# Gathering the overflow rows of four experts as one group of 128

## The chip, the cores and the metric

One Trainium2 chip, of which this kernel uses one core. The core has TensorE (matrix products, with a separate instruction that loads the stationary operand), VectorE, ScalarE, GpSimd and SyncE, which run their own instruction streams and wait for each other through semaphores, and 16 DMA engines. The metric is the device time of one launch in microseconds (us). An engine name in a profile row is short: PE is TensorE's products, PEld its loads of stationary operands, DVE is VectorE, ACT ScalarE, POOL GpSimd, SP SyncE.

## The reference, cut to what matters

One decoder layer on 1024 tokens of width 1024: forgetting attention, a layer norm, a mixture of experts, a layer norm. The change touches the mixture of experts: 64 experts, 8 for each token, each with a gate and an up matrix of 1024 x 256 and a down matrix of 256 x 1024, and one shared expert of the same size that takes all tokens.

```python
def moe(x, w_router, router_bias, w_gate, w_up, w_down, ws_gate, ws_up, ws_down):
    ...
    _, top_e = lax.top_k(jnp.where(exp_mask, sel, -jnp.inf), TOP_K)
    w = jnp.take_along_axis(scores, top_e, axis=-1)
    w = w / jnp.sum(w, -1, keepdims=True) * ROUTED_SCALE
    ...
    # for each block of rows of one expert e:
        xb = x_pad[rows]
        h = jax.nn.silu(xb @ w_gate[e]) * (xb @ w_up[e])
        yb = (h @ w_down[e]) * rw[:, None].astype(xb.dtype)
        acc = acc.at[rows].add(yb)
    shared = (jax.nn.silu(xf @ ws_gate) * (xf @ ws_up)) @ ws_down
```

An expert has 128 tokens on the mean (8192 choices, 64 experts), some have more and some fewer.

## The kernel before, in words

All products are made in a split form: a float32 operand is written as a high part (what the product's number format keeps) and a low part (the rest), and a product is the sum of high x high, high x low and low x high. The high part is a copy on ScalarE, the low part a subtraction on VectorE.

**Tables.** After routing, every choice of a token is written into a table in device memory (`tab_dram`). For each expert the table has a column for its first 128 tokens and then columns for blocks of 32 further tokens; a column stands for 128 rows of which a further block uses 32. `TAB_BLOCKS` = 29 columns lie side by side for each expert (`e * TAB_BLOCKS + k`), and SyncE reads the whole table into SBUF (L548, 928 KB). Places of no token hold the numbers of rows that are zero. `further` has the number of further blocks of each expert, `earlier` the number of further blocks of all experts before it.

**One expert.** GpSimd gathers its 128 rows (1024 values and 64 token weights for each, 4352 bytes) with an indirect DMA (L657) some three experts ahead. TensorE turns them (eight transposes, L1015), ScalarE and VectorE split them (L1424, L1922). The weights come by plain DMA in four pieces for gate and up (L493) and two for down (L498), 512 KB each, are split piece by piece (L1396 on ScalarE, L1918 on VectorE), and are held in two sets. TensorE makes the gate and up products in 16 + 8 matmuls (`gate_up`, L1025, L1028, L1031), two transposes of h (L1039), and the down product in 12 (`down`, L1052, L1053, L1060). ScalarE scales the result by the tokens' weights (L1444), and GpSimd adds it to the sums in device memory with an accumulating indirect DMA (`add_first`, L682). Each add waits for the add before it.

**A further block** of 32 rows is gathered on its own (`gather_further`, L670), turned on its own (`turn_further`, eight transposes, L1074), copied into `xo` by ScalarE (`further_rows_hi`, L1486) and VectorE (`further_rows_lo`, L1938): columns 0 to 31 of `xo` are the high part, 32 to 63 the low part, the rest is zero. Then TensorE makes 16 matmuls with the same gate and up weights (`gate_up_further`, L1084, L1085), and in the next expert two transposes (L1093) and eight matmuls of the down product (L1102, L1103).

**The order on TensorE**, written out by hand, for expert e (m = e + 8, since the shared expert's eight tiles come first): transposes of h of e - 1; gate and up of e; if e - 1 had a further block, its two transposes; the turning of the rows of e + 1 into `q_ps`; if e - 1 had a further block, its down product; if e has one, its turning; the down product of e - 1 into `k_ps`; if e has a further block, its gate and up product. ScalarE and VectorE follow the same order: of the four weight pieces of a coming expert VectorE does three, then h of e, then the fourth, then the split of the next rows, then the two pieces of the down weights. The loops of the engines have two experts in a turn. In the end the last expert's results are not added through memory but placed by TensorE (L1118 to L1128), together with a second layer norm.

Of the kernel before, what the change touches and what calls it, by code (L numbers as in the profile page):

```python
# [73 lines left out]
XR = P // 4  # L74

# [20 lines left out]
def build(nc, x, w_in, b_f, w_out, ln1_g, ln1_b, router, router_bias, w_gate, w_up, w_down, ws_gate, ws_up,  # L96
          ws_down, ln2_g, ln2_b, out):
    with ExitStack() as ctx:
# [135 lines left out]
        with ExitStack() as m:  # L234
# [6 lines left out]
            xo = sb("xo", [P, DC, P], F32R, c=m)  # L241
# [16 lines left out]
            tab = sb("tab", [P, TAB], I32, c=m)  # L258
            tok_f = sb("tok_f", [P, 1], c=m)
            tok_x = sb("tok_x", [2 * XR, 1], c=m)  # L260
        with ExitStack() as f:
# [18 lines left out]
            sb("up_to_the_other_set", [P, 19240], c=f)  # L280
# [5 lines left out]
        for n in ("masks xt_ps xt_hi_ok xt_lo_ok wf_in wf_ok gate_ps g1_in gate_step zexp_ok"  # L286
# [7 lines left out]
                  " ht_lo_ok downed scaled w_ok x_in x_turned x_rows_hi_ok x_rows_lo_ok x_w_ok x_gated x_half x_sum x_silu_ok x_h_ok x_ht_ps x_ht_hi_ok x_ht_lo_ok"  # L294
                  " x_downed x_y_half x_scaled ax_ok ax_stored summed"
                  " stands std_ok var_ok place_step y_hi_ok f_placed f_pair f_mean f_var f_std f_scaled f_step f_xg f_out").split():
# [17 lines left out]
        w_rows = w_in.rearrange("(c p) n -> p c n", p=P)  # L314
        v_rows = v_dram.rearrange("(t p) h n -> p t h n", p=P)
# [64 lines left out]
        def _(sp):  # L380
# [166 lines left out]
            sp.wait_ge(S["extra_ok"], 2)  # L547
            sp.dma_start(tab[:], tab_dram.rearrange("(p n) o -> p (n o)", p=P)).then_inc(S["c_loads"], 16)  # L548
# [36 lines left out]
        def _(pool):  # L585
# [27 lines left out]
            g.iota(e8[:], pattern=[[TAB_BLOCKS, E]], base=1, channel_multiplier=0, allow_small_or_imprecise_dtypes=True).then_inc(S["c_const"], 1)  # L613
# [26 lines left out]
            def wait_routed():  # L640
                pool.wait_ge(S["listed"], 16 * TT * TOP_K)
                pool.wait_ge(S["extra_ok"], 2)
                pool.wait_ge(S["x1_stored"], 16 * TT)
                pool.wait_ge(S["wts_stored"], 16 * TT)

            def gather(i, e, count, free):
# [5 lines left out]
                g.tensor_copy(gidx[i][:], tab[:, ds(e * TAB_BLOCKS, 1)]).then_inc(idx_ok[i], 1)  # L652
# [19 lines left out]

            def add_first(par, e):
# [3 lines left out]
                g.tensor_copy(sidx[par][:], tab[:, ds(e * TAB_BLOCKS, 1)]).then_inc(S["sidx_ok"], 1)  # L677
# [7 lines left out]
            def add_further(e, k, x):  # L685
                pool.wait_ge(sent[2], 16 * x + SENT_0[2])
                stand(pool)
                g.tensor_copy(sidx[2][0:XR], tab[0:XR, ds(e * TAB_BLOCKS + k + 1, 1)]).then_inc(S["x_sidx_ok"], 1)
# [4 lines left out]
                                     in_=ys[2][0:XR], in_offset=None, compute_op=ALU.add).then_inc(sent[2], 16)  # L693

            def earlier_of(e):
                return pool.value_load(earlier[0:1, ds(e + 1, 1)], min_val=0, max_val=E * TAB_BLOCKS)

# [3 lines left out]
            for b in range(SH):  # L701
# [11 lines left out]
            f0, f1 = further_of(0), further_of(1)  # L713
            with pool.If(f0 > 0):
                gather_further(0, 0, 0, 0)
            with pool.If(f0 < 2):
# [1438 lines left out]
```

## Time and profile before

| | |
|---|---|
| median of 3 runs | 1633.97 us (1632.95 to 1635.86) |
| the profiled execution | 1633.34 us, span of its instructions 1631.7 us |
| TensorE | busy 1567.5 us (96%) |
| TensorE's loads | 1309.8 us (80%) |
| VectorE | 1178.9 us (72%) |
| ScalarE | 1033.5 us (63%) |
| GpSimd | 506.6 us (31%) |
| data moved by DMA | 368.63 MB |

Busy time is the union of the instructions' times on that engine. Matmuls are pipelined: a matmul of 512 columns is shown with about 0.39 us, while the next one begins 0.23 us after it. Expert 0 begins at 752 us of the span, expert 63 at 1568.

### The profile page before, as it was taken

Reading aid. Unit: us, or ns where it says so; the run is one execution under the profiler, and the core shown is the slowest. Engines: PE = TensorE matmul, PEld = TensorE weight load, DVE = VectorE, ACT = ScalarE, POOL = GpSimd, SP = SyncE. Lnnn points to the kernel's source line nnn. Section 1 sums busy time; section 2 is a strip of 40 time slices with the busy share of each in tenths; the row PEclk is TensorE's granted clock in tenths of the full one; section 3 lists DMA queues with packets and bytes.
Section 4 is the critical chain, followed back from the end, with each engine's and each line's share of the span. In section 5 each row is a group of like instructions: output and inputs, shape, how many; then the busy total and the mean of one; then the engine's idle time right before and its main releaser. Section 6 shows DMA issues by size and latency. Waiting matters only on the chain.

```text
span 1631.7 us, 32189 instructions
## 1 busy us (share of the span) xinstructions
PE 1567.5 (96%) x8246; PEld 1309.8 (80%) x8247; DVE 1178.9 (72%) x2037; ACT 1033.5 (63%) x1706; POOL 506.6 (31%) x495
## 2 busy tenths in 40 slices
PE   6999999999999999989999999999999999999986
PEld 6897888888887788778888888888888888888763
DVE  4215777777777788836877787777876787888866
ACT  3215666666666654526777787767776777878754
POOL 0000000000000125532554454543454454454426
PEclk9999999999999999999999999999999999999995
DMA  7223322222123434557999999999999999999987
GB/s 246 91 81 91 72 53 65 58 64 71 45 71 104 161 144 146 221 192 267 330 312 323 304 354 366 342 289 274 333 328 286 286 358 327 352 367 362 368 250 281
DMA packets 161321, 368.63 MB, mean 226 GB/s; under 512 B 53010, under 2 KB 73490, under 8 KB 161266
## 3 DMA queue, kind: packets, MB, share of 16 engines
q1 hardware_dynamic: 136272, 284.21, 49.7%
q0 software_dynamic: 24992, 83.73, 19.7%
q8 instruction: 28, 0.46, 0.1%
q14 instruction: 29, 0.22, 0.0%
HBM read 294.39 MB, written 65.11 MB: 220 GB/s over the span
## 4 chain that ended last, share of the span: by engine, by line
PE 73%; DVE 8%; DMA 7%; issue 5%; ACT 3%; ACTq 2%; POOL 1%; SPq 0%; DVEq 0%; POOLq 0%
PE bank_pair L1031 6%; PE bank_pair L1025 6%; PE bank_pair L1028 6%; DMA sums_scratch<-ys,sidx 6%; PE q_ps L91 4%; PE q_ps L93 4%; PE q_ps L92 4%; PE out_ps L916 4%; PE k_ps L894 3%; PE out_ps L1084 3%; PE out_ps L1085 3%; PE q_ps L1015 3%; PE k_ps L1052 2%; PE k_ps L1053 2%; PE k_ps L1060 2%
## 5 line engine op out<-in xcount | busy, mean ns | idle before, releaser
L1918 DVE TENSOR_TENSOR gu_lo<-raw_gu,gu_hi 128x1024 fp32r<-128x1024 f32 x260 | 306.4, 1220 | 28.0 <-ACT gu_hi L1396 27.8
L1396 ACT CAST gu_hi<-raw_gu 128x1024 fp32r<-128x1024 f32 x260 | 253.6, 1049 | 7.1 <-DMA raw_gu<-in_moe_w_up_dram 7.1
L1025 PE MATMUL bank_pair<-gu_hi,xb_hi 128*128 128x512 f32 x576 | 233.9, 406 | 5.3 <-DVE gu_lo L1918 3.9
L1028 PE MATMUL bank_pair<-gu_lo,xb_hi 128*128 128x512 f32 x576 | 227.7, 395 | 0.0
L682 POOL DMA_INDIRECT sums_scratch<-ys,sidx x63 | 120.8, 1917 | 152.9 <-DMA sums_scratch<-ys,sidx 118.9
L1918 DVE TENSOR_TENSOR dn_lo<-raw_dn,dn_hi 128x1024 fp32r<-128x1024 f32 x130 | 152.6, 1213 | 2.8 <-ACT dn_hi L1396 2.3
L1031 PE MATMUL bank_pair<-gu_hi,xb_lo 128*128 128x512 f32 x576 | 144.0, 392 | 3.8 <-DVE xb_lo L1922 3.8
L1025 PEld LDWEIGHTS bank_pair<-gu_hi,xb_hi 128*128 128x128 f32 x576 | 110.6, 192 | 28.6 <-issue 5.8
L613 POOL IOTA e<- 128x64 f32 x1 | 0.2, 185 | 427.5 <-DVE xs L1714 427.5
L1396 ACT CAST dn_hi<-raw_dn 128x1024 fp32r<-128x1024 f32 x130 | 130.0, 1052 | 4.2 <-DMA raw_dn<-in_moe_w_down_dram 4.2
L1301 ACT CAST pt_hi<-k_ps 128x512 fp32r<-128x512 f32 (+1 forms) x192 | 85.8, 482 | 73.5 <-PE k_ps L894 72.8
L1031 PEld LDWEIGHTS bank_pair<-gu_hi,xb_lo 128*128 128x128 f32 x576 | 108.5, 188 | 26.9 <-DVE xb_lo L1922 4.3
L1028 PEld LDWEIGHTS bank_pair<-gu_lo,xb_hi 128*128 128x128 f32 x576 | 110.1, 191 | 21.3
L657 POOL DMA_INDIRECT x_rows<-rows_scratch,gidx x64 | 80.5, 1258 | 140.7 <-DVE wcol L1934 109.1
L1692 DVE TENSOR_TENSOR pt_lo<-k_ps,pt_hi 128x512 fp32r<-128x512 f32 (+1 forms) x192 | 100.3, 550 | 27.4 <-ACT pt_hi L1301 26.6
L1052 PE MATMUL k_ps<-dn_hi,ht_hi 128*128 128x512 f32 x288 | 118.3, 411 | 0.0
L1053 PE MATMUL k_ps<-dn_lo,ht_hi 128*128 128x512 f32 x288 | 112.6, 391 | 0.0
L91 PE MATMUL q_ps<-xt_hi,wqk_hi 128*128 128x512 f32 x256 | 108.8, 425 | 0.0
L1290 ACT ACTIVATE probs<-bank_pair,nm 128x512 f32<-128x512 f32 (+3 forms) x128 | 74.8, 587 | 43.2 <-DVE nm L1685 29.8
L1084 PE MATMUL out_ps<-gu_hi,xo 128*128 128x512 f32 x248 | 97.3, 392 | 4.8 <-DVE xo L1938 4.8
L93 PE MATMUL q_ps<-xt_hi,wqk_lo 128*128 128x512 f32 x256 | 100.3, 392 | 0.0
L92 PE MATMUL q_ps<-xt_lo,wqk_hi 128*128 128x512 f32 x256 | 100.0, 391 | 0.0
(307 smaller groups left out, 3967.5 us busy)
## 6 DMA issues: line engine op xcount, KB each, us to landing
raw_gu<-in_moe_w_gate_dram SPq DMA_DIRECT2D x128, 512.0 KB, 7.0
raw_gu<-in_moe_w_up_dram SPq DMA_DIRECT2D x128, 512.0 KB, 9.1
raw_dn<-in_moe_w_down_dram SPq DMA_DIRECT2D x128, 512.0 KB, 8.7
wqk<-in_fox_w_in_dram SPq DMA_DIRECT2D x66, 128.0 KB, 2.5
v_scratch<-v_out SPq DMA_DIRECT2D x32, 256.0 KB, 2.8
va<-v_scratch SPq DMA_DIRECT2D x16, 512.0 KB, 4.6
fin<-sums_scratch SPq DMA_DIRECT2D x16, 512.0 KB, 9.5
xs<-in_x_dram SPq DMA_DIRECT2D x8, 512.0 KB, 7.3
```

Source lines behind the costliest of these rows:

```text
L91: pe.matmul(out, w_hi, m_hi, start=start, stop=False, skip_group_check=True)
L92: pe.matmul(out, w_hi, m_lo, start=False, stop=False, skip_group_check=True)
L93: return pe.matmul(out, w_lo, m_hi, start=False, stop=stop, skip_group_check=True)
L682: g.indirect_dma_start(out=sums[0], out_offset=bass.IndirectOffsetOnAxis(ap=sidx[par][:, 0:1], axis=0), in_=ys[par][:], in_offset=None, co ...
L1025: i = pe.matmul(o3, xb_hi[s][:, c], g_hi[:, :, c], start=c == 0, stop=False, skip_group_check=True)
L1028: pe.matmul(o3, xb_hi[s][:, c], g_lo[:, :, c], start=False, stop=False, skip_group_check=True)
L1031: i = pe.matmul(o3, xb_lo[s][:, c], g_hi[:, :, c], start=False, stop=c == DC - 1, skip_group_check=True)
L1052: pe.matmul(k_ps[:, r], ht_hi[:, c], d_hi[:, c, r], start=c == 0, stop=False, skip_group_check=True)
L1053: pe.matmul(k_ps[:, r], ht_hi[:, c], d_lo[:, c, r], start=False, stop=False, skip_group_check=True)
L1084: pe.matmul(o3, xo[:, c], g_hi[:, :, c], start=c == 0, stop=False, skip_group_check=True)
L1396: a.copy(hi, raw).then_inc(S[done], 1)
L1918: dve.tensor_tensor(lo, raw, hi, ALU.subtract).then_inc(S[lo_ok], 1)
```

## The change

The first further blocks of four consecutive experts are one group. GpSimd gathers 4 x 32 rows with one indirect DMA of 128 rows (`gather_four`), for each of the 16 groups, whether its experts have a further block or not; places of no block read the zero rows. In the first expert of a group (j = 0) TensorE turns all 128 rows with the eight full transposes into `k_ps` (`turn_four`), between the eighth and the ninth matmul of gate and up; before that it waits for the gather and for the scaling that last read `k_ps`. ScalarE copies the high part between its third and fourth weight piece (`rows_of_four_hi`), VectorE subtracts the low part after its third piece and copies the four columns of weights (`rows_of_four_lo`), and TensorE waits for that before it writes `k_ps` again in the down product. `xo` now holds all four experts, each as 32 columns of high and 32 of low part for each of the eight chunks; the stationary operand of a further product is 128 columns from the expert's place on, so that its last 64 columns are rows of a neighbour, whose results nobody reads. Second and later further blocks of an expert go another way (`gather_again`, `turn_again`), with their table column read from device memory.

The table is laid out by block (column `k * E + e`), so that only its first 128 columns, 64 KB, are read into SBUF. VectorE makes one more running sum (`again`, second and later blocks) and four small copies that put the groups' indices together (`fidx`). The loops have four experts in a turn. Several semaphores are merged.

```diff
-            xg = [sb(f"x_rows{i}", [P, ROW_W], c=m) for i in range(3)]
+            xg = [sb(f"x_rows{i}", [P, ROW_W], c=m) for i in range(2)]
+            xgx = sb("x_rows_of_four", [P, ROW_W], c=m)
...
-            ys = [sb(f"ys{i}", [P, D], c=m) for i in range(3)]
+            ys = [sb(f"ys{i}", [P, ROW_W if i == 2 else D], c=m) for i in range(3)]
+            xr = ys[2][XR:2 * XR]
...
-            tab = sb("tab", [P, TAB], I32, c=m)
+            tab = sb("tab", [P, 2 * E], I32, c=m)
+            xo = sb("xo", [P, DC * 2 * P + 2 * XR], F32R, c=m)
+            xo_of = xo[:, 0:DC * 2 * P].rearrange("p (c j s r) -> p c j s r", j=FOUR, s=2, r=XR)
+            fidx = sb("fidx", [P, E // FOUR], I32, c=m)
+            fidx_g = sb("fidx_g", [P, 1], I32, c=m)
+            w_four = sb("w_four", [P, FOUR], c=m)
+            again = sb("again", [1, E + 1], I32, c=m)
...
-            sp.dma_start(tab[:], tab_dram.rearrange("(p n) o -> p (n o)", p=P)).then_inc(S["c_loads"], 16)
+            sp.wait_ge(S["extra_ok"], 3)
+            sp.dma_start(tab[:], tab_rows[:, 0:2 * E]).then_inc(S["c_loads"], 16)
...
-            g.iota(e8[:], pattern=[[TAB_BLOCKS, E]], base=1, channel_multiplier=0, allow_small_or_imprecise_dtypes=True).then_inc(S["c_const"], 1)
+            g.iota(e8[:], pattern=[[1, E]], base=1, channel_multiplier=0, allow_small_or_imprecise_dtypes=True).then_inc(S["c_const"], 1)
...
-            def gather_further(par, e, k, x):
-
-                if not static(x):
-                    with pool.If(x > 0):
-                        pool.wait_ge(S["x_in"], 16 * x)
-                        stand(pool)
+            def gather_four(n):
+
+                if static(n) and n == 0:
+                    pool.wait_ge(S["extra_ok"], 3 + FOUR)
+                else:
+                    pool.wait_ge(S["fx_lo_ok"], 2 * n)
                 stand(pool)
-                g.tensor_copy(gidx[2][0:XR], tab[0:XR, ds(e * TAB_BLOCKS + k + 1, 1)]).then_inc(idx_ok[2], 1)
-                pool.wait_ge(idx_ok[2], x + 1)
+                g.tensor_copy(fidx_g[:], fidx[:, ds(n, 1)]).then_inc(idx_ok[2], 1)
+                pool.wait_ge(idx_ok[2], n + 1)
                 stand(pool)
-                g.indirect_dma_start(out=xg[2][par * XR:(par + 1) * XR], out_offset=None, in_=rows_dram,
+                g.indirect_dma_start(out=xgx[:], out_offset=None, in_=rows_dram,
+                                     in_offset=bass.IndirectOffsetOnAxis(ap=fidx_g[:, 0:1], axis=0)).then_inc(S["fx_in"], 16)
+
+            def gather_again(e, k, n):
+
+                pool.wait_ge(S["x_rows_lo_ok"], n + 1)
+                stand(pool)
+                pool.dma_start(gidx[2][0:XR], tab_rows[0:XR, ds((k + 1) * E + e, 1)], allow_slow_non_contiguous=True).then_inc(S["x_in"], 16)
+                pool.wait_ge(S["x_in"], 32 * n + 16)
+                stand(pool)
+                g.indirect_dma_start(out=xr, out_offset=None, in_=rows_dram,
                                      in_offset=bass.IndirectOffsetOnAxis(ap=gidx[2][0:XR, 0:1], axis=0)).then_inc(S["x_in"], 16)
...
+            gather_four(0)
...
+                if j == 1 and not (static(four) and four == E // FOUR - 1):
+                    gather_four(four + 1)
...
                 with pool.If(nx > 1):
-                    with pool.Fori(1, nx) as k:
-                        pool.wait_ge(S["x_w_ok"], xi + k + 1)
-                        gather_further(par, e, k, xi + k)
-                        add_further(e, k - 1, xi + k - 1)
-                    if not ends:
-                        with pool.If(f1 > 0):
-                            gather_further(1 - par, e + 1, 0, xi + nx)
-                if pos != "last":
-                    with pool.If(f1 < 2):
-                        with pool.If(f2 > 0):
-                            pool.wait_ge(S["x_w_ok"], xi + nx + 1)
-                            gather_further(par, e + 2, 0, xi + nx + f1)
+                    n = again_of(e)
+                    sums_rows(first_of_further(e), xi)
+                    add_further(xi)
+                    gather_again(e, 1, n)
+                    with pool.If(nx > 2):
+                        with pool.Fori(2, nx) as k:
+                            sums_rows(gidx[2][0:XR], xi + k - 1)
+                            add_further(xi + k - 1)
+                            gather_again(e, k, n + k - 1)
...
+            def gate_up(s, w, names, n, between=None):
...
+                    if between and c == DC // 2 - 1:
+                        between()
...
-            def turn_further(par, x):
-
-                pe.wait_ge(S["x_in"], 16 * x + 16)
+            def turn_four(n, m):
+
+                pe.wait_ge(S["fx_in"], 16 * n + 16)
+                pe.wait_ge(S["scaled"], m - 1)
                 stand(pe)
-                rows = slice(par * XR, (par + 1) * XR)
-                v = strided(xg[2][rows, 0:D])
+                turn_rows(xgx, k_ps).then_inc(S["fx_turned"], 1)
...
-                pe.wait_ge(S["x_rows_lo_ok"], x + 1)
                 pe.wait_ge(S["x_scaled"], x + 1)
                 for c in range(DC):
-                    pe.matmul(o3, xo[:, c], g_hi[:, :, c], start=c == 0, stop=False, skip_group_check=True)
-                    i = pe.matmul(o3, xo[:, c], g_lo[:, :, c], start=False, stop=c == DC - 1, skip_group_check=True)
-                i.then_inc(S["x_gated"], 1)
+                    rows = xo[:, (FOUR * c + j) * 2 * XR:(FOUR * c + j) * 2 * XR + P]
+                    pe.matmul(o3, rows, g_hi[:, :, c], start=c == 0, stop=False, skip_group_check=True)
+                    i = pe.matmul(o3, rows, g_lo[:, :, c], start=False, stop=c == DC - 1, skip_group_check=True)
+                i.then_inc(S["x_product"], 1)
...
+                between = None if j else rows_of_four
...
+                if j == 0:
+                    pe.wait_ge(S["fx_lo_ok"], 2 * four + 1)
+                    stand(pe)
                 with pe.If(nx > 0):
                     with pe.If(nx > 1):
+                        n = pe.value_load(again[0:1, ds(e, 1)], min_val=0, max_val=E * TAB_BLOCKS)
+                        pe.wait_ge(S["ht_lo_ok"], m)
+                        stand(pe)
                         with pe.Fori(0, nx - 1) as k:
-                            pe.wait_ge(S["ht_lo_ok"], m)
-                            turn_further(par, xi + k)
-                            gate_up_further(w, xi + k)
+                            gate_up_further(w, j, xi + k)
                             turn_h_further(xi + k)
                             down_further(w, e + 2, xi + k)
-                    pe.wait_ge(S["ht_lo_ok"], m)
-                    turn_further(par, xi + nx - 1)
+                            turn_again(n + k)
+                            pe.wait_ge(S["x_rows_lo_ok"], n + k + 2)
+                            stand(pe)
                     down(m - 1, par, e + 1)
                     if last:
...
+                        next_gate_up(m, e, par, range(G_PIECES - 1))
+                    if j == 0:
+                        rows_of_four_hi(four)
+                    if pos != "last":
+                        next_gate_up(m, e, par, range(G_PIECES - 1, G_PIECES))
...
+            def rows_of_four_hi(n):
+                act.wait_ge(S["fx_turned"], n + 1)
+                a.copy(xo[:, 0:DC * 2 * P].rearrange("p (q s r) -> p q s r", s=2, r=XR)[:, :, 0], k_ps[:].rearrange("p (q r) -> p q r", r=XR)
+                       ).then_inc(S["fx_hi_ok"], 1)
...
-                step(dve.tensor_tensor(pos_b[:], pos_b[:], e8[:], ALU.add))
+                step(dve.scalar_tensor_tensor(out=pos_b[:], in0=pos_b[:], scalar=float(E), in1=e8[:], op0=ALU.mult, op1=ALU.add))
...
+                step(dve.tensor_scalar(u[:], nblk_i[1][:], float(-(P // XR) - 1), 0.0, ALU.add, ALU.max))
+                shift = 1
+                while shift < E:
+                    step(dve.tensor_copy(v[:, 0:shift], u[:, 0:shift]))
+                    step(dve.tensor_tensor(v[:, shift:E], u[:, shift:E], u[:, 0:E - shift], ALU.add))
+                    u, v = v, u
+                    shift *= 2
+                step(dve.memset(again[:], 0))
+                dve.tensor_copy(again[:, 1:E + 1], u[:]).then_inc(S["extra_ok"], 1)
...
-            def further_rows_lo(par, e, x):
-                dve.wait_ge(S["x_rows_hi_ok"], x + 1)
-                dve.tensor_tensor(xo[:, :, XR:2 * XR], banks[1][:, FF:FF + DC * XR].rearrange("p (c t) -> p c t", c=DC), xo[:, :, 0:XR],
+            def rows_of_four_lo(n):
+                dve.wait_ge(S["fx_hi_ok"], n + 1)
+                q = xo[:, 0:DC * 2 * P].rearrange("p (q s r) -> p q s r", s=2, r=XR)
+                dve.tensor_tensor(q[:, :, 1], k_ps[:].rearrange("p (q r) -> p q r", r=XR), q[:, :, 0], ALU.subtract).then_inc(S["fx_lo_ok"], 1)
+                dve.tensor_copy(w_four[:], xgx[:, ds(FOUR * n + D, FOUR)]).then_inc(S["fx_lo_ok"], 1)
+
+            def first_weights(j, four):
+                dve.wait_ge(S["fx_lo_ok"], 2 * four + 2)
+                stand(dve)
+                dve.tensor_copy(w_x[:], w_four[j * XR:(j + 1) * XR, j:j + 1])
...
+                    dve.wait_ge(S["c_loads"], 64)
+                    for j in range(FOUR):
+                        dve.tensor_copy(fidx[j * XR:(j + 1) * XR], tab[0:XR, E + j:2 * E:FOUR]).then_inc(S["extra_ok"], 1)
...
+            with pe.Fori(0, E // FOUR - 1) as i:
+                for j in range(FOUR):
+                    expert(FOUR * i + j, j, i)
```

## Rows read from the trace of the kernel before

**Rows 1.** Windows of the expert stage: length, busy time per engine, clock, DMA share, GB/s.
```profile
785.00:1385.00 600.00, 594.86 (x2918) 496.29 (x2917) 465.64 (x594) 436.40 (x571) 292.52 (x282) 1.00 0.99 320
1385.00:1485.00 100.00, 99.06 (x486) 83.15 (x485) 84.91 (x105) 79.09 (x101) 49.08 (x45) 1.00 1.03 355
1485.00:1505.00 20.00, 19.54 (x96) 16.36 (x95) 16.92 (x21) 16.94 (x21) 10.01 (x9) 1.00 1.03 385
```

**Rows 2.** The chain that ended last, from 1480 on: first and last of ten adds.
```profile
1490.46 9.38 DMA sums_scratch<-ys,sidx
...
1583.15 6.24 DMA sums_scratch<-ys,sidx
```

**Rows 3.** ScalarE: the rows of expert 62 are scaled.
```profile
1577.63 1.12 ACT L1444 ACTIVATE ys<-k_ps,wcol 128x1024 f32<-128x1024 f32 x1 [0.80 <-PE k_ps L1060]
```

**Rows 4.** View of the tile xo: durations, first and last start; who waited.
```profile
L1084 PE MATMUL out_ps<-gu_hi,xo x248: 387/389/504, 781.8 to 1580.8; 128*128 128x512 f32 x124
...
  PE out_ps L1084: 4.8, 6
```

**Rows 5.** TensorE in order of time, experts 12 and 15: start, length, line.
```profile
914.75 0.48 PE L1025 MATMUL bank_pair<-gu_hi,xb_hi 128*128 128x512 f32 x1
...
920.30 1.05 PE L1015 MATMUL q_ps<-ident,x_rows 128*128 128x128 f32 x8
921.11 0.48 PE L1052 MATMUL k_ps<-dn_hi,ht_hi 128*128 128x512 f32 x1
...
923.03 1.08 PE L1060 MATMUL k_ps<-dn_hi,ht_lo 128*128 128x512 f32 x4
...
949.73 1.05 PE L1015 MATMUL q_ps<-ident,x_rows 128*128 128x128 f32 x8
950.71 1.06 PE L1074 MATMUL bank_pair<-ident,x_rows 32*128 32x32 f32 x8
...
953.65 1.07 PE L1060 MATMUL k_ps<-dn_hi,ht_lo 128*128 128x512 f32 x4
954.56 0.39 PE L1084 MATMUL out_ps<-gu_hi,xo 128*128 128x512 f32 x1
```

**Rows 6.** The same at expert 6, whose further rows are late.
```profile
839.30 1.07 PE L1060 MATMUL k_ps<-dn_hi,ht_lo 128*128 128x512 f32 x4
841.24 0.50 PE L1084 MATMUL out_ps<-gu_hi,xo 128*128 128x512 f32 x1 [0.87 <-DVE xo L1938]
```

**Rows 7.** Groups by line, 800 to 1550: a full 128-row split on VectorE.
```profile
L1922 DVE TENSOR_TENSOR xb_lo<-q_ps,xb_hi 128x1024 fp32r<-128x1024 f32 x57 | 69.4, 1218 | 0.0
```

**Rows 8.** TensorE, expert 16 (further block before it): its gate and up product starts.
```profile
958.35 0.48 PE L1025 MATMUL bank_pair<-gu_hi,xb_hi 128*128 128x512 f32 x1
```

**Rows 9.** VectorE, the same expert: its three weight pieces.
```profile
961.12 3.50 DVE L1918 TENSOR_TENSOR gu_lo<-raw_gu,gu_hi 128x1024 fp32r<-128x1024 f32 x3 [0.47 <-ACT gu_hi L1396]
```

**Rows 10.** TensorE, expert 48 (no further block before it).
```profile
1396.25 0.48 PE L1025 MATMUL bank_pair<-gu_hi,xb_hi 128*128 128x512 f32 x1
```

**Rows 11.** VectorE, expert 48: its three weight pieces.
```profile
1401.33 3.50 DVE L1918 TENSOR_TENSOR gu_lo<-raw_gu,gu_hi 128x1024 fp32r<-128x1024 f32 x3 [0.52 <-ACT gu_hi L1396]
```

**Rows 12.** TensorE, expert 0.
```profile
752.08 0.48 PE L1025 MATMUL bank_pair<-gu_hi,xb_hi 128*128 128x512 f32 x1
```

**Rows 13.** GpSimd at that time: the gather for expert 2.
```profile
755.07 1.00 POOL L657 DMA_INDIRECT x_rows<-rows_scratch,gidx  x1 [0.86 <-POOL gidx L652]
```

**Rows 14.** View of the tile x_rows, 755 to 757: that gather alone.
```profile
DMA to landing us min/median/max: 5.6/5.6/5.6
```

**Rows 15.** Windows around a stop of TensorE, columns as in the first group.
```profile
703.00:707.00 4.00, 0.47 (x3) 0.04 (x1) 1.04 (x2) 0.00 (x0) 0.29 (x2) 1.00 0.97 331
707.00:711.00 4.00, 3.69 (x13) 2.94 (x14) 0.80 (x3) 0.39 (x1) 3.08 (x4) 0.66 0.09 30
```

**Rows 16.** View of the tile raw_gu, 1385 to 1420: weight pieces.
```profile
DMA to landing us min/median/max: 8.3/13.6/19.9
```

**Rows 17.** Groups by line, VectorE, 714 to 719: the running sum of block counts.
```profile
L1909 DVE TENSOR_TENSOR nblk<-nblk 1x63 f32<-1x63 f32 (+5 forms) x6 | 1.2, 203 | 0.2
```

More of the change, by code:

```diff
@@ L74 @@
 XR = P // 4
+FOUR = P // XR
 BIAS_TILES = TT // 2
@@ L762, in expert @@
                 return xi, nx
-            expert(0, 0, "first")
-            expert(1, 1, "")
-            with pool.Fori(1, E // 2 - 2) as i:
-                for par in range(2):
-                    expert(2 * i + par, par, "")
-            expert(E - 4, 0, "")
-            expert(E - 3, 1, "", ahead=False)
-            expert(E - 2, 0, "last", ahead=False)
-            xi, nx = expert(E - 1, 1, "last", ahead=False)
+            for j in range(FOUR):
+                expert(j, j, 0, "" if j else "first")
+            with pool.Fori(1, E // FOUR - 1) as i:
+                for j in range(FOUR):
+                    expert(FOUR * i + j, j, i, "")
+            for j in range(FOUR):
+                expert(E - FOUR + j, j, E // FOUR - 1, "" if j < 2 else "last", ahead=j < 1)
             for what, t in LAST_POOL:
@@ L1163, in _, with expert @@
                     logits(TT - 1)
-            def expert(e, par, last=False):
+            def expert(e, j, four, last=False):
+                par = j % 2
                 w = 1 - par
@@ L1217, in expert @@
                 return xi, nx
-            with pe.Fori(0, E // 2 - 1) as i:
-                for par in range(2):
-                    expert(2 * i + par, par)
-            expert(E - 2, 0)
-            expert(E - 1, 1, last=True)
+            with pe.Fori(0, E // FOUR - 1) as i:
+                for j in range(FOUR):
+                    expert(FOUR * i + j, j, i)
+            for j in range(FOUR):
+                expert(E - FOUR + j, j, E // FOUR - 1, last=j == FOUR - 1)
         @block.scalar
@@ L1514, in load_counts, with expert @@
                 return [act.value_load(earlier[0:1, ds(e + k, 1)], min_val=0, max_val=E * TAB_BLOCKS) for k in range(4)]
-            def expert(e, par, pos, counts):
+            def expert(e, j, four, pos, counts):
+                par = j % 2
                 m = SH + e
@@ L1585, in expert, with four_experts @@
                     a.copy(bank_pair[:], b2[:]).then_inc(S["y_hi_ok"], 1)
-            counts = load_counts(0)
-            expert(0, 0, "first", counts)
-            expert(1, 1, "", counts)
-            with act.Fori(1, E // 2 - 1) as i:
-                counts = load_counts(2 * i)
-                for par in range(2):
-                    expert(2 * i + par, par, "", counts)
-            counts = load_counts(E - 2)
-            expert(E - 2, 0, "", counts)
-            expert(E - 1, 1, "last", counts)
+            def four_experts(e0, four):
+                for j in range(FOUR):
+                    if j % 2 == 0:
+                        counts = load_counts(e0 + j)
+                    pos = "first" if static(e0) and e0 + j == 0 else "last" if static(e0) and e0 + j == E - 1 else ""
+                    expert(e0 + j, j, four, pos, counts)
+            four_experts(0, 0)
+            with act.Fori(1, E // FOUR - 1) as i:
+                four_experts(FOUR * i, i)
+            four_experts(E - FOUR, E // FOUR - 1)
             for t in range(TT):
@@ L2007, in load_counts, with expert @@
                 return [dve.value_load(earlier[0:1, ds(e + k, 1)], min_val=0, max_val=E * TAB_BLOCKS) for k in range(4)]
-            def expert(e, par, counts, last=False):
+            def expert(e, j, four, counts, last=False):
+                par = j % 2
                 m = SH + e
```

175 lines of the change are left out of this document (98 added, 77 removed).

## The prediction

> **What bounds the kernel now.** The change works in the expert stage alone, so I read that stage first: the windows from 785 to 1385 and from 1385 to 1485 [rows 1]. TensorE is busy for 595 of 600 us and for 99 of 100 at full clock, VectorE and ScalarE for 70 to 85%. Busy time of a pipelined engine proves little alone, so I then read TensorE's timeline, where a missing matmul shows as a start that is late. There the matmuls follow each other at their usual distance, with few stops. So in this stage TensorE's instruction stream sets the time, and a microsecond less on it is worth one, as long as nothing else comes up behind it. Two things stand close behind. DMA has a share of 0.99 to 1.03 and moves 320 to 385 GB/s [rows 1]; and from 1490 us on the chain that ended last has left TensorE and is ten accumulating adds, one after the other, 9.4 us for the first, to 1589.4 [rows 2]. The rows of expert 62 are scaled at 1578.75 [rows 3], and their add starts at 1583.15, because the one before it has only then landed: 4.4 us of slack for TensorE. So the end of the stage is set by when that chain starts, and what TensorE saves or loses after expert 53 is not on the path.
>
> How many blocks there are: 248 matmuls of L1084, eight for each block, are 31 blocks [rows 4]. In TensorE's timeline each of the 31 groups is followed by the next expert's products, none by a second block of the same expert. So the new way for second blocks (a table column from memory, a gather behind a finished add) is never taken here, and costs nothing.
>
> **What goes.** The 32-row turning. Compare expert 12, which has no block, with expert 15, which has one [rows 5]: from the first transpose of the next rows to the low part of the down product it takes 923.03 - 920.30 = 2.73 us without and 953.65 - 949.73 = 3.92 with it. So one turning costs 1.19 us of TensorE, more than its eight transposes' distance, since the engine also drains and waits around it. It is no cheaper for having 32 rows: the full turning of 128 rows takes 921.11 - 920.30 = 0.81. Thirty of the 31 stand ahead of the adds' chain (the last one is expert 63's): 30 x 1.19 = 35.7 us. With it goes a stall: the further product waits for the split rows. At expert 6 it starts 1.94 us after the low part of the down product [rows 6] against 0.91 at expert 15 [rows 5], so a shown wait of 0.87 costs 1.03. Six such waits sum to 4.8 us [rows 4], which is 4.8 x 1.03 / 0.87 = 5.7 us. The new split is done long before. Together 41.4 us go.
>
> **What comes on TensorE.** One full turning for each group, 14 of them up to expert 52. The bare turning is 0.81 [rows 5], the inserted small one with its wait 1.19; the new one has a wait ahead and a second wait before the down product. At expert 15 a turning with a wait starts 0.98 after the one before it, in place of 0.81 [rows 5], so a wait costs 0.17 and the top is 1.36. I take 1.3, near the top because both waits are there: 14 x 1.3 = 18.2 us (bounds 11.3 and 19.0).
>
> **The wait before the down product.** It releases when VectorE has split the group: 1.22 us [rows 7] after its third weight piece. Behind the waiting TensorE stand the down product, the scaling and the add of the expert before. Down is due 5.55 us after gate and up start (914.75 to 920.30), plus 0.81 for the next rows [rows 5], plus 1.2 for the new turning: 7.56. Where the expert before had a block (10 of the 14), two transposes and eight matmuls of 0.24 come between as well, and it is due after 9.7. In expert 16, such a one, the products start at 958.35 [rows 8] and the three pieces end at 964.6 [rows 9], so the split ends 7.5 us in: no wait. Where it had none, VectorE starts later: in expert 48 the products start at 1396.25 [rows 10], the pieces run from 1401.33 to 1404.83 [rows 11], the split ends at 1406.0, and down is due at 1403.8. That is 2.2 us of waiting, for experts 12, 44 and 48 (56 and 60 lie in the adds' chain; expert 0 follows below). A part comes back, since in such stretches TensorE waits for VectorE at the next product anyway. Between 0 and 2.2 I take 1.5: 4.5 us.
>
> **The first group.** This is late at once. Expert 0 starts at 752.08 [rows 12], so its eighth matmul is over at 754.0. GpSimd issues the first group's gather only after the shared expert's last stores, in the place where today the gather for expert 2 stands, at 755.07 [rows 13]; that one landed 5.6 us later [rows 14], at 760.7. TensorE stands still for 6.7 us, with ScalarE and VectorE queued behind the same rows. After a stop of under 4 us the granted clock of the next 4 us was 0.66 of 2.4 GHz, so partly its 1.2 GHz level, and 1.00 before [rows 15]; 0.34 x 4 is 1.4 us more. Sum 8.1, bounds 0 (if the gather went out ahead) and 10.
>
> **DMA.** A group moves 128 x 4352 = 0.557 MB, a block today 0.139; in all 16 x 0.557 - 31 x 0.139 = 4.6 MB more. From 785 to 1385 I let them pass, since the cover is the weights' double buffer. From 1385 to 1485 a weight piece takes up to 19.9 us to land [rows 16], when two experts without blocks, at some 9.3 us each (914.75 to 923.03 and four matmuls more [rows 5]), are the time it has. There two groups more and three blocks fewer are 0.70 MB, at 355 GB/s [rows 1] 2.0 us. The bounds are 0 and all 4.6 MB, 13 us.
>
> Here the windows show 355 GB/s over 100 us and 385 over 20 [rows 1]. The Trainium skill ("DMA: Bandwidth & Descriptors", section Bandwidth) puts the share of device memory's bandwidth that a core has at about 358 GB/s, which speaks against a change that moves more. The 385 are above it over a short stretch, so it is no hard wall here; taken as one, those 0.70 MB cost 2.0 us too, and the whole 4.6 MB 12.9, the fourth case below.
>
> **At no cost.** ScalarE gives 30 small copies and gets 14 large ones, VectorE 14 splits of 1.22 [rows 7] for 30 smaller ones; both are idle for 15 to 30% of the stage [rows 1], and where they are late is costed above. The second running sum is some fourteen instructions like those of the first, 203 ns each [rows 17], under 4 us, in the shared expert's tiles, where VectorE waits for TensorE's next product; without that cover it would be those 4 us. The smaller table, read well before its use, the same number of table operations and the merged semaphores change no path. GpSimd has 15 gathers fewer and stays off the path.
>
> **Sum.** 41.4 - 18.2 - 4.5 - 8.1 - 2.0 = 8.6 us less. From the profiled execution's 1633.3 that is 1624.7; the median of the runs shown is 0.6 above it: 1625.
>
> **Rivals.** 0.2% is 3.3 us, about what a measurement of this kernel can tell from no change.
> 1. As summed: 1625, between 1618 and 1630. Chance 0.50.
> 2. More of it stays: a bare turning (11.3), no wait for the split, no DMA loss, the first stop as costed: 41.4 - 11.3 - 8.1 = 22 us, 1612; with the costed turning 1619. For it: expert 16 has 2.2 us to spare [rows 8, 9]. Against it: the wait in expert 48 is worked out from starts that I have no reason to doubt. Between 1611 and 1618: 0.16.
> 3. Slower: TensorE waits before the down product in all 14 groups, because ScalarE's copy between its third and fourth piece pushes VectorE's pieces back even where a block came before. At 2.2 us each that is 30.8 in place of 4.5: 1651. It decides from 0.94 us for each group on (8.6 + 4.5 over 14). Against it: the same 2.2 us of expert 16. Chance 0.17, of which 0.05 within 0.2%.
> 4. DMA keeps what TensorE gives: the 4.6 MB show whole, 13 us in place of 2: 1636. For it: the landing times and the share of 1.03. Against it: up to 1385 all waits together, for weights or else, leave TensorE idle for 5 of 600 us [rows 1], and the slack of 4.4 us ahead of the last adds takes up as much. Chance 0.17, of which 0.07 is a milder form, still faster.
>
> Faster by over 0.2%: 0.50 + 0.16 + 0.07 = 0.73; within: 0.05 + 0.10 = 0.15; slower 0.12. The range leaves out the deep ends of the second and third case, 1612 to 1636; the likeliest case alone is 1618 to 1630.
>
> **What would show it.** L1074 gone and 16 more groups of eight transposes, each in the middle of a gate and up product, about 1.3 us from matmul to matmul; no wait for xo before L1084; a stop of 6 to 7 us in expert 0, with a lower clock behind it; in experts 12, 44 and 48 a wait of about 2 us before L1052 for the group's split, none in 16. The chain's adds start some 9 us earlier and take as long as now. Wrong it would be if the first stop is hidden, if waits stand before L1052 in most groups, or if ScalarE begins to wait for raw weights before 1480.

## The result, and the profile after

The change made the kernel slower: 1736.99 us (median of 4 runs, 1732.82 to 1738.59) against 1633.46 (4 runs, 1630.55 to 1635.86), a ratio of 1.0631 with a 95% interval of 1.0605 to 1.0657. That is 103.5 us more, where 8.6 fewer were forecast.

The windows of [rows 1], now of the kernel after (length, then busy time of TensorE, its loads, VectorE, ScalarE and GpSimd, clock, DMA share, GB/s):

```profile
785.00:1385.00 600.00, 542.99 (x2529) 450.84 (x2529) 427.08 (x537) 392.03 (x502) 215.66 (x227) 0.95 0.92 296
1385.00:1485.00 100.00, 89.40 (x432) 74.67 (x430) 72.06 (x85) 67.19 (x83) 41.76 (x39) 0.95 0.95 309
```

Every engine is less busy than before, DMA too. So nothing has become the bound by doing more work: something stands still. The page says it in two of its parts, the chain that ended last and the DMA queues (packets, MB, share):

```profile
q14 instruction: 170, 1.39, 0.2%
q8 instruction: 34, 0.56, 0.1%
...
PE 61%; issue 13%; DVE 10%; DMA 7%; ACT 4%; DVEq 2%; POOL 2%; ACTq 1%; SPq 0%; POOLq 0%
```

"issue" is time in which an engine waited for nothing that the profile shows. It was 5% of the chain before and is 13% now: some 225 us against 82. And one of the two queues that bring instructions, q14, carried 170 packets and not 29. Two of these lines as they were before:

```profile
q14 instruction: 29, 0.22, 0.0%
...
PE 73%; DVE 8%; DMA 7%; issue 5%; ACT 3%; ACTq 2%; POOL 1%; SPq 0%; DVEq 0%; POOLq 0%
```

Where the standing still lies, the waits by engine and line from 757 to 1690 show (us in total, times, longest). TensorE first, then ScalarE, then VectorE:

```profile
PE k_ps L1077 <- DVE w_four L2001: 41.5, 5, 10.5
PE out_ps L1134 <- DVE ho L2025: 39.6, 11, 3.9
PE out_ps L1125 <- DVE gu_x L2020: 14.0, 10, 2.1
PE k_ps L1038 <- DMA x_rows_of_four<-rows_scratch,fidx_g: 7.2, 1, 7.2
```

```profile
ACT gu_x L1537 <- issue: 65.0, 9, 7.6
...
ACT ht_hi L1473 <- issue: 49.1, 15, 8.0
```

```profile
DVE gu_x L2016 <- ACT gu_x L1537: 101.1, 29, 7.9
...
DVE gu_x L2016 <- issue: 16.2, 2, 8.4
DVE ht_lo L1991 <- issue: 8.6, 1, 8.6
```

TensorE's waits sum to 102 us, and all but the first group's 7.2 end at VectorE. A reader who stops there concludes that the group's split (`w_four` is its last instruction) is the culprit. But VectorE waits for ScalarE, and ScalarE for "issue". The same in order of time at expert 12, the first of its four: ScalarE, then VectorE, then TensorE.

```profile
938.37 1.12 ACT L1485 ACTIVATE ys<-k_ps,wcol 128x1024 f32<-128x1024 f32 x1
947.06 0.37 ACT L1473 CAST ht_hi<-bank_pair 128x256 fp32r<-128x256 f32 x1 [7.58 <-issue]
```

```profile
937.67 2.36 DVE L1979 TENSOR_TENSOR dn_lo<-raw_dn,dn_hi 128x1024 fp32r<-128x1024 f32 x2
948.66 0.42 DVE L1991 TENSOR_TENSOR ht_lo<-bank_pair,ht_hi 128x256 fp32r<-128x256 f32 x1 [8.62 <-issue]
```

```profile
939.98 1.05 PE L1038 MATMUL k_ps<-ident,x_rows_of_four 128*128 128x128 f32 x8
940.79 0.48 PE L1048 MATMUL bank_pair<-gu_hi,xb_hi 128*128 128x512 f32 x1
...
944.53 1.05 PE L1038 MATMUL q_ps<-ident,x_rows 128*128 128x128 f32 x8
954.54 0.79 PE L1077 MATMUL k_ps<-dn_hi,ht_hi 128*128 128x512 f32 x1 [8.96 <-DVE w_four L2001]
955.13 0.63 PE L1078 MATMUL k_ps<-dn_lo,ht_hi 128*128 128x512 f32 x1
955.56 0.63 PE L1077 MATMUL k_ps<-dn_hi,ht_hi 128*128 128x512 f32 x1
```

ScalarE and VectorE both stop right after the last work of expert 11, before they have touched anything of the group. That is the turn of their loops: the change made a turn of four experts out of two, since the group's work stands in the first of four. From the down product on, TensorE's matmuls follow each other after 0.43 us, not 0.23: after it has stood still for 9 us, its granted clock is 0.50 from 954.5 to 960, the lower level of 1.2 GHz, and 0.97 in the 5 us after that.

```profile
954.50:960.00 5.50, 5.46 (x13) 4.20 (x14) 4.12 (x5) 1.08 (x2) 2.48 (x2) 0.50 0.77 268
```

### The profile page after: what moved, and what is told of

Its sections match the earlier page's. It is cut to its first block, busy times and chain, and to the rows that moved or that the text cites. A ratio compares the mean times of both kernels' runs of the same rounds, so it can differ in the third digit from the quotient of the medians.

```text
span 1734.6 us, 31066 instructions
## 1 busy us (share of the span) xinstructions
PE 1580.9 (91%) x8126; PEld 1319.6 (76%) x8127; DVE 1193.3 (69%) x2057; ACT 1035.2 (60%) x1691; POOL 458.5 (26%) x465
## 3 DMA queue, kind: packets, MB, share of 16 engines
q14 instruction: 170, 1.39, 0.2%
## 4 chain that ended last, share of the span: by engine, by line
PE 61%; issue 13%; DVE 10%; DMA 7%; ACT 4%; DVEq 2%; POOL 2%; ACTq 1%; SPq 0%; POOLq 0%
PE bank_pair L1056 4%; DMA sums_scratch<-ys,sidx 4%; PE bank_pair L1048 4%; PE bank_pair L1051 4%; PE out_ps L939 4%; PE q_ps L92 4%; PE q_ps L94 3%; PE q_ps L93 3%; PE k_ps L917 3%; PE k_ps L1077 2%; PE k_ps L1078 2%; DVE gu_lo L1979 2%; PE out_ps L1134 2%; PE q_ps L1038 2%; PE out_ps L1117 2%
## 5 line engine op out<-in xcount | busy, mean ns | idle before, releaser
L1077 PE MATMUL k_ps<-dn_hi,ht_hi 128*128 128x512 f32 x288 | 123.1, 427 | 41.5 <-DVE w_four L2001 41.5
L701 POOL DMA_INDIRECT sums_scratch<-ys,sidx x63 | 115.4, 1832 | 155.6 <-DMA sums_scratch<-ys,sidx 106.4
L1078 PE MATMUL k_ps<-dn_lo,ht_hi 128*128 128x512 f32 x288 | 118.0, 410 | 0.0
L2016 DVE TENSOR_TENSOR gu_x<-out_ps,gu_x 32x512 f32<-32x512 f32 x31 | 21.1, 680 | 117.3 <-ACT gu_x L1537 101.1
L1077 PEld LDWEIGHTS k_ps<-dn_hi,ht_hi 128*128 128x128 f32 x288 | 58.7, 204 | 54.8 <-issue 42.4
```

What stands on the lines that cost most here:

```text
L701: g.indirect_dma_start(out=sums[0], out_offset=bass.IndirectOffsetOnAxis(ap=sidx[par][:, 0:1], axis=0), in_=ys[par][:], in_offset=None, co ...
L1077: pe.matmul(k_ps[:, r], ht_hi[:, c], d_hi[:, c, r], start=c == 0, stop=False, skip_group_check=True)
L1078: pe.matmul(k_ps[:, r], ht_hi[:, c], d_lo[:, c, r], start=False, stop=False, skip_group_check=True)
```

## The experiments

e1, e2 and e9 to e11 were run six or ten times each, the others once; what the single runs decide are differences of some 90 us and more.

**The theory and its rivals.** Theory: the jump back to the loop's start makes the stop. The loop's body (the instructions of one turn) has grown, its first instructions are no longer at hand when the engine jumps back, and it waits until they are fetched. Rivals: the group's own work (copy and split of 128 rows, and the waits around it) makes the stop; or the gathered rows or the weights land late.

**e1: the loops of ScalarE and VectorE written out**, no jump back, everything else as in the change.

```diff
-            with act.Fori(1, E // FOUR - 1) as i:
+            for i in range(1, E // FOUR - 1):
                 four_experts(FOUR * i, i)
...
-            with dve.Fori(0, E // FOUR - 1) as i:
+            for i in range(E // FOUR - 1):
                 four_experts(FOUR * i, i)
```

> The changed kernel with the expert loops of ScalarE and VectorE written out (no jump back; TensorE's and GpSimd's loops stay at four experts a turn). Loop theory: the stop of 7 to 8.6 us that ScalarE and VectorE make at every fourth expert, waiting for nothing that the trace shows, is the jump back of a loop whose body of four experts has grown too long (ScalarE 145 to 328 instructions, VectorE 165 to 370); some 14 such stops are the 103 us that the change lost. Without the jump they go: 1610 to 1640 us, and no wait of TensorE for VectorE's w_four of 9 to 10 us is left. First rival, the group's own work (the copy and the split of 128 rows at the first of four experts, and their waits) makes the stop: all of that stays here, so 1725 to 1745 us. Second rival, the gathered rows or the weights land late: stays as well, 1725 to 1745 us. Against the loop theory in a third way: code that runs once must all be fetched, so stops of the same size would stand along the whole stretch and the time would be above 1737.

Measured: 1627.03 us, 0.9962 of the kernel before [0.9949, 0.9976]. The long stops are gone (the longest "issue" row of ScalarE and VectorE in the expert stage is 1.8 us), and the kernel is 110 us faster than the change while it does the same work in the same order. Both rivals fall. Code that runs once does not stop either, although the instruction queue carries 86 packets.

**e2: two experts a turn again** on ScalarE and VectorE, the group's copy and split behind a test; GpSimd and TensorE stay at four.

```diff
+                    with dve.If(h < 1):
+                        rows_of_four_lo(four)
...
             with dve.Fori(0, E // FOUR - 1) as i:
-                four_experts(FOUR * i, i)
+                with dve.Fori(0, 2) as h:
+                    counts = load_counts(FOUR * i + 2 * h)
+                    for par in range(2):
+                        expert(FOUR * i + 2 * h + par, par, i, counts, h=h)
...
```

> The changed kernel with ScalarE's and VectorE's loops back at two experts a turn (the group's copy and split behind a test for the first pair of the four); TensorE and GpSimd stay at four. Body of ScalarE's loop 185 instructions, of VectorE's 237, against 328 and 370. Loop theory: the long stops go and what is left is what the two-expert loops cost in the kernel before, some 2 us a turn, most of it hidden: 1615 to 1645 us. Rivals (the group's work, late rows): 1725 to 1745 us.

Measured: 1637.54 us, 1.0020 [1.0007, 1.0034]. The long stops are gone here too. It is 10 us above e1; what the tests and the second loop cost was not followed up.

**e3: the kernel before, its two loops at four experts a turn**, nothing else.

```diff
-            with dve.Fori(0, E // 2 - 1) as i:
-                counts = load_counts(2 * i)
-                for par in range(2):
-                    expert(2 * i + par, par, counts)
+            with dve.Fori(0, E // 4 - 1) as i:
+                for j in range(4):
+                    if j % 2 == 0:
+                        counts = load_counts(4 * i + j)
+                    expert(4 * i + j, j % 2, counts)
...
```

> The kernel before, with nothing changed but that ScalarE's and VectorE's loops hold four experts a turn (bodies of 284 and 326 instructions against 145 and 165); no group of 128 rows, no new gathers. Loop theory: stops of 7 to 9 us at every fourth expert, 1633 plus 80 to 115: 1710 to 1750 us. Rivals (the group's work, late rows): nothing of theirs is here, 1625 to 1640 us.

Measured: 1631.16 us, no stops, 32 packets. This is a miss for the theory as I had put it: four experts in a turn is not enough.

**e4: the change without the branches that these inputs never enter.** Left out on ScalarE and VectorE: the work for a second further block of an expert.

```diff
-                with dve.If(nx > 1):
-                    n = dve.value_load(again[0:1, ds(e, 1)], min_val=0, max_val=E * TAB_BLOCKS)
-                    first_weights(j, four)
...
```

> The changed kernel, four experts a turn, but without the parts of ScalarE's and VectorE's loops for a second further block of an expert, which these inputs never enter (no expert has two): that work is left out. Bodies 231 and 258 instructions against 328 and 370. Loop theory, if the length of the body decides: ScalarE's stops go and VectorE's go or shrink, 1620 to 1690 us. Loop theory, if what counts is that four experts are in a turn and not the length: 1725 to 1745. Rivals (the group's work, late rows): 1725 to 1745 us.

Measured: 1630.72 us, no stops, 32 packets. Code that never runs had cost 106 us. So the length or the place of the body decides. e5 to e8 were to tell which, and whose stop counts.

**e5: the change, its loops moved** by a block that is never entered; **e6: e3, its loops moved** in the same way (64 copies here on VectorE and 82 on ScalarE), so that they end where those of the change end. VectorE's part of e5:

```diff
+            with dve.If(dve.value_load(earlier[0:1, ds(1, 1)], min_val=0, max_val=E * TAB_BLOCKS) > E * TAB_BLOCKS - 1):
+                for _ in range(120):
+                    dve.tensor_copy(hh[:], sg[:])
             with dve.Fori(0, E // FOUR - 1) as i:
```

> The changed kernel, four experts a turn, bodies as long as in the change (308 instructions on ScalarE and 346 on VectorE without the labels), but with a block of 120 instructions that is never entered ahead of each of the two loops, so that the same loop stands 124 instructions later in the engine's program. So far bodies of 260 and 302 did not stop (e3_before_four) and 308 and 346 did. If the length of the body decides (a limit between 302 and 346 on VectorE, between 260 and 308 on ScalarE): the stops stay, 1725 to 1745 us. If the place decides, that is how far the loop's end stands in the block in which code is fetched: the stops go or change their size, 1615 to 1640 us if they go.

> The kernel before with four experts a turn on ScalarE and VectorE as in e3_before_four (bodies 260 and 302), and a block that is never entered (82 and 64 instructions) ahead of each loop, so that both loops end about where those of the changed kernel end (instruction 1224 and 1257 of the engine's program, against 1222 and 1255). If length decides: no stops, 1625 to 1640 us as in e3_before_four. If the place of the loop's end decides: stops of 7 to 9 us a turn as in the changed kernel, 1710 to 1750 us.

Measured: e5 1734.38 us, e6 1779.52. e5 alone would have said "length". e6 says that it can't be: its bodies are those of e3, instruction for instruction, and 148 us slower by their place alone. VectorE's waits in e6, from 757 to 1740, and its queue:

```profile
DVE gu_x L1955 <- issue: 117.5, 10, 13.4
...
DVE ht_lo L1941 <- issue: 49.0, 5, 13.2
```

```profile
q14 instruction: 103, 0.84, 0.1%
```

ScalarE's long stops are absent in e6 (its largest "issue" row there is 22.8 us in 13, the longest 2.6): only VectorE's loop had moved to a bad place.

**e7 and e8: the change with one of the two loops written out.**

> The changed kernel with ScalarE's loop alone written out; VectorE's stays at four experts a turn. Tells whose stop carries the time. If VectorE's alone is enough (its stop of 8.6 us stands ahead of w_four and the split that TensorE waits for): 1715 to 1740 us. If ScalarE's is what delays both: 1620 to 1640. If each delays the other by its own: in between, near 1680.

> The changed kernel with VectorE's loop alone written out; ScalarE's stays at four experts a turn. If VectorE's stop carries the time: 1620 to 1640 us. If ScalarE's does: 1715 to 1740. If both stop at the same time and either is enough: 1700 to 1740 here and in e7_unroll_act.

Measured: 1734.17 and 1724.58 us. Either engine's stops are enough. VectorE's loop jumps back 14 times, ScalarE's 13: against e1, (1734.2 - 1627.0) / 14 = 7.7 us and (1724.6 - 1627.0) / 13 = 7.5 us for each jump. VectorE's own rows in e7 count the same 14 stops, 7.6 us each on the mean:

```profile
DVE gu_x L2016 <- issue: 74.7, 10, 8.4
...
DVE ht_lo L1991 <- issue: 32.1, 4, 9.0
```

In the change both stop at once, so the price is paid once.

**Worked out from these eight.** The packets of that queue are 1.39 MB / 170 = 8.2 KB, and an instruction of the built program has 64 bytes: a piece of 128 instructions. I asked whether one set of borders, 128 apart, puts every loop that stopped across three borders and every other across two at most. It does, if they lie at 61 to 66 beyond a multiple of 128, the same on both engines (first and last instruction of the body, counted in the built program without labels; borders with 64):

```
kernel          ScalarE                    VectorE
before          770 to  902, 1 border      888 to 1040, 1
e2              915 to 1087, 1             910 to 1126, 2
e3              879 to 1138, 2             888 to 1189, 2
e4              831 to 1049, 2             910 to 1151, 2
after           915 to 1222, 3  stops      910 to 1255, 3  stops
e5             1039 to 1346, 3  stops     1034 to 1379, 3
e6              965 to 1224, 2             956 to 1257, 3  stops
e7              written out                910 to 1255, 3  stops
e8              915 to 1222, 3  stops      written out
e9, predicted   999 to 1306, 2             980 to 1325, 2
e12, predicted 1007 to 1266, 2            1016 to 1317, 2
```

In e5 VectorE's stops can't be told from its waits for ScalarE; that its 173 packets are about as many as the change's 170 says that it fetches as well. The move of 124 in e5 was unluckily almost one whole piece. That makes two predictions: the change cured by a move of half a piece, and e3 left alone by a move of a whole one.

**e9: the change, moved by 84 (ScalarE) and 70 (VectorE); e12: e3 moved by 128.** The diffs are those of e5 and e6, with other numbers.

> The changed kernel with its loops as long as they are (308 and 346 instructions), moved by a block that is never entered so that they begin 84 instructions later on ScalarE and 70 later on VectorE; nothing else is changed. The theory so far: code comes in pieces of some 8 KB (the extra packets of the instruction queue are 8.2 KB each: 128 instructions of 64 bytes), and a jump back finds its target still there if the loop lies across no more than two borders of pieces. From the loops that stopped and those that did not, the borders are worked out: in the change both loops lie across three, here across two. So no stops: 1622 to 1640 us, and some 30 packets in that queue instead of 170. If it is length that decides, or if only some other distance from the program's start does: stops as before, 1725 to 1745 us.

> The kernel before with four experts a turn (bodies 260 and 302), moved by 128 instructions on both engines, one whole piece by the theory; e6_before_four_shift moved them by 86 and 68 and took 1779.5 us. If the place within a piece of 128 decides: no stops, as without the move, 1625 to 1640 us. If any move of this kind, or the block that is never entered, brings the stops, or the borders are 256 apart: 1700 to 1790 us.

Measured: e9 1627.89 us, 0.9961 [0.9946, 0.9975]; e12 1630.43. Both as predicted. In e9 the loops are as long as in the change and hold the same instructions, and a few dozen that are never run, ahead of them, are worth 109 us. The queue, and TensorE's waits from 757 to 1690:

```profile
q14 instruction: 37, 0.30, 0.1%
```

```profile
PE k_ps L1077 <- DVE w_four L2004: 13.7, 5, 2.9
PE k_ps L1038 <- DMA x_rows_of_four<-rows_scratch,fidx_g: 6.6, 1, 6.6
```

170 - 37 is 133 packets for 27 jumps back, 4.9 each; e6 against e12 is 70 for 14, 5.0 each. What is left without stops is every piece once: the built programs of ScalarE, VectorE, GpSimd and SyncE together make 37.1 pieces of 128 instructions in e9 and 87.1 in e1, and the queue carried 37 and 86 packets.

The Trainium skill ("Runtime: NRT & Kernel Launch", section Instruction fetch mechanics) says that most engines hold 512 instructions (TensorE 2048), filled in order in blocks of 256, and that a taken branch whose target is outside that window has to wait for a fetch. The runs agree that a jump back can wait for its target. A loop that stopped lies in four pieces, 512 instructions: as much as that window, and still its start was not at hand. The Trainium skill and the runs differ in the grain for ScalarE and VectorE: packets of 8.2 KB, and borders 128 apart fit where 256 apart do not. The same ScalarE loop of 308 instructions stops at 915 and at 1039; wherever one set of borders 256 apart may lie, it does not put the loop across two of them both times, and across one the loop always lies, at 999 too, where it does not stop. Packets of 256 instructions do stand on the page of the profile, in the other queue, q8: 34 of 16.5 KB in the change, in e1 and in e9, and TensorE's 8717 instructions make 34.05 pieces of 256.

**e10 and e11: the first group's gather earlier**, in e9 and in e1. GpSimd issues it before its wait for the last but one tile's scaled rows.

```diff
                     gather(b % 2, b + 2 - SH, 0, [(S["turned"], b + 1)])
+                if b == SH - 1:
+                    gather_four(0)
...
-            gather_four(0)
             gather(0, 2, 1, [(S["w_ok"], 1)])
```

> As e9_shift70, and GpSimd issues the first group's gather in the last shared block before its wait for ScalarE's scaled rows, some 7 us earlier. The stop of TensorE in the gate and up product of expert 0 (7.2 us in the changed kernel, 5.8 with the loops written out) goes: 6 to 9 us less than e9_shift70, 1614 to 1630. If that stop only uncovers another wait (for the weights of expert 1 or the rows of expert 2): within 2 us of e9_shift70.

> As e1_unrolled (both loops written out), with the same earlier gather of the first group. If the stop in expert 0 was worth its length: 1627 less 5 to 8, 1618 to 1623 us. If it only uncovers another wait: 1625 to 1629.

Measured: e10 1627.49 us, 0.9943 [0.9924, 0.9962]; e11 1625.17, 0.9934 [0.9916, 0.9952], the lowest median of all. The intervals overlap those of e9 and e1, so an effect of the earlier gather is not shown. I had expected the stop to go, and it did not: in e10 TensorE's wait shrank from 6.6 to 3.7 only. The gather was issued about 3 us before TensorE's product of expert 0 began and took 8.5 us to land.

```profile
755.80 1.13 POOL L679 DMA_INDIRECT x_rows_of_four<-rows_scratch,fidx_g  x1 [0.83 <-POOL fidx_g L676]
```

## Why the prediction was wrong

**The step that failed** is "At no cost". It weighed what ScalarE and VectorE do in a turn and not what a turn is: the loops go from two experts to four, with new branches for second blocks, and the body on VectorE from 153 instructions to 346. No rival had the loop in it either. The cover that I named, engines idle for 15 to 30% of the stage, does not help: a stop of 7.5 us at one place is longer than the slack of any one expert. What stood in place of "no cost" are 14 stops of 7.5 to 7.7 us, some 107 of the 110 us between the change and e1.

**The third rival named the wrong place and the wrong cause.** TensorE waits before the down product for the split in five groups only, in the change (41.5 us in all) as in e9 (13.7, with the stops gone). In the ten groups that follow an expert with a block, TensorE stands still in the change earlier, at that block's transposes and down product (L1125 and L1134, some 53 us together), because ScalarE and VectorE have stopped. And ScalarE's copy does not push VectorE's pieces back where a block came before: in e9 no such wait stands there.

**The other terms**, as e9 shows them without the stops. The 32-row turnings and the waits for xo are gone: at experts with a block it is 2.73 us from the turning of the next rows to the low part of the down product (expert 2: 789.28 to 792.01), as in expert 12 of [rows 5], and 0.91 to the further product. The first group's stop was right: 6.6 us in e9 and 7.2 in the change against 6.7 forecast. The lower clock behind it costs more, 2.3 us and not 1.4: the eight transposes take 1.60 us in place of 0.81, and expert 0 is 9.85 us longer than before, of which the stop is 6.6 and a turning 0.9. The inserted turning costs 0.90 elsewhere (0.81 to the next matmul, and the one after that comes 0.32 and not 0.23 later), near the lower bound and not 1.3: for 14 of them 5.6 us less than the sum had. The wait before the down product was too small: expert 12 in e9,

```profile
926.25 1.05 PE L1038 MATMUL q_ps<-ident,x_rows 128*128 128x128 f32 x8
930.10 0.49 PE L1077 MATMUL k_ps<-dn_hi,ht_hi 128*128 128x512 f32 x1 [2.81 <-DVE w_four L2004]
```

and it stands at experts 12, 44, 48, 56 and 60, 13.7 us in all, 8.4 of them in the three that I had put at 4.5. None stands at expert 16. The 2 us for DMA are not seen: neither TensorE nor ScalarE waits for weights in e9. These misses go both ways; that the sum of 8.6 us comes out near what is measured without the stops is in part luck. The last add of the chain begins 5.3 us earlier than in [rows 2], although expert 0 begins 3.1 us later than in [rows 12],

```profile
1577.88 6.18 DMA sums_scratch<-ys,sidx
```

and e1 and e9, at 1627.0 and 1627.9 us, are 7 and 6 us below the kernel before as measured with them, where 8.6 were forecast.

**Open.** Expert 0 began between 752.1 and 754.0 us in the profiled runs of the four kernels without the group (before, e3, e6, e12) and between 751.0 and 759.9 in the ten with it, 3.3 us later on the mean. The clock in the 20 us from 660 to 680, where the tokens are routed, was 0.83 in all of those four and 0.74 in seven of these ten; whether the changed table arithmetic causes it was not tested. And VectorE's stops in e6 are longer than 7.6 us: 14 at the turns, 10.3 to 13.4 us each, 165.0 in all, 11.8 on the mean (the fifteenth of its rows is 1.5 us, behind the loop); why was not tested.

## What to carry to other kernels

A loop's body is a resource like a buffer: when a change makes a turn do more, count the instructions of the turn on every engine, the branches that never run included, and look for engines that stop at the turn with "issue" as the releaser and for a growing instruction queue. Follow a wait back to the engine that waits for nothing before you blame the instruction that released it. By this fit a body of at most 256 instructions, which can't lie across three borders 128 apart, would be safe wherever it stands; that was not tested as such. A longer one has to be placed, or written out, which cost nothing here.

## What the runs showed of the hardware

A jump back whose loop lay across three borders of pieces of 128 instructions, as worked out above, cost 7.5 to 7.7 us with the change's loops (e7, e8) and 10.6 in e6 (148.4 / 14, 11.8 of standing still), with about five packets of 8.2 KB in the instruction queue each time. Two engines that stop at the same jump pay once. The same loop of 346 instructions cost nothing at 980 and 7.7 us a turn at 910. Code written out to over 4700 instructions an engine made no such stop.
